# Another order for the last stage of the first pass, with six of eight next-norm tiles turned by DMA, filler products in the head, and the first weights loaded in two halves

## Time and profile before

| | us |
|---|---|
| three timed runs | 1172.57, 1175.30, 1181.07 (median 1175.3) |
| the profiled execution | 1170.05 |
| its span, slowest core (core 2) | 1168.3 |
| spans of the eight cores | 1163.5 to 1168.3 |
| granted TensorE clock, mean of each core | 0.996 to 0.998 |

### The profile page before, as it was taken

The page is one execution under the profiler, slowest core; times in us unless marked ns, Lnnn a source line. Parts: engine busy times, 40 slices in busy tenths (PEclk is TensorE's granted clock), DMA queues, the critical chain, the costliest instruction groups (busy, mean ns, idle before and its releaser), DMA issues.

```text
span 1168.3 us, 18289 instructions; the slowest of 8 cores (1163.5 to 1168.3 us)
## 1 busy us (share of the span) xinstructions
PE 1124.1 (96%) x6425; PEld 574.5 (49%) x6520; DVE 609.8 (52%) x668; ACT 384.7 (33%) x649; POOL 341.8 (29%) x451
## 2 busy tenths in 40 slices
PE   4999999999999999999899999999999999999996
PEld 2444454444444444443446666666644444444443
DVE  3267662123687776124615866322267888871247
ACT  3622221111354444014772223112133444430134
POOL 2411113222234434114832010222223333330144
PEclk9999999999999999999999999999999999999998
DMA  7983642544844333358699355244377343343443
GB/s 185 183 158 72 111 71 46 80 83 78 145 93 72 73 73 72 62 92 192 196 195 233 63 116 90 37 73 73 72 127 127 73 73 73 73 90 64 79 102 129
DMA packets 58585, 119.77 MB, mean 103 GB/s; under 512 B 33264, under 2 KB 34032, under 8 KB 55936
## 3 DMA queue, kind: packets, MB, share of 16 engines
q0 software_dynamic: 20112, 82.85, 40.9%
q1 hardware_dynamic: 38240, 35.58, 11.3%
q10 hardware_dynamic: 144, 0.17, 0.1%
HBM read 184.14 MB, written 9.95 MB: 166 GB/s over the span
## 4 chain that ended last, share of the span: by engine, by line
PE 88%; POOL 3%; issue 2%; DVE 2%; DMA 2%; ACT 1%; DVEq 0%; POOLq 0%; ACTq 0%; SPq 0%
PE pq L322 88%; POOL s_wd L335 2%; DMA s_ring<-wpk 1%; DVE s_wd L338 1%; ACT s_xnb L329 1%; POOL s_st_r L335 1%; POOL s_st_ss L335 1%; DMA s_h<-x 1%; ACT s_wd L329 0%; DVE s_h L338 0%; PE pq L326 0%; POOL s_R L335 0%; DVE s_xnb L510 0%; DVE s_xnb L338 0%; DVE s_xn L335 0%
## 5 line engine op out<-in xcount | busy, mean ns | idle before, releaser
L322 PE MATMUL pq<-s_xn,s_ring 128*128 128x512 bf16 (+3 forms) x3693 | 658.1, 334 | 4.2 <-DVE s_wd L338 0.8
L322 PEld LDWEIGHTS pq<-s_xn,s_ring 128*128 128x128 bf16 x3744 | 335.6, 98 | 313.2 <-issue 2.0
L338 DVE SCALAR_TENSOR_TENSOR s_wd<-pq,s_cst,s_wd 128x1023 f32<-128x1023 f32 (+1 forms) x176 | 225.2, 1282 | 63.1 <-ACT s_carry_f L332 53.8
L335 POOL TENSOR_TENSOR s_R<-s_wd 128x1024 bf16<-128x1024 f32 (+3 forms) x84 | 146.3, 1742 | 357.9 <-DVE s_wd L338 166.6
L322 PE MATMUL pq<-s_ring,s_R 128*128 128x512 bf16 x936 | 206.9, 379 | 2.7 <-DVE s_wd L338 1.4
L338 DVE SCALAR_TENSOR_TENSOR s_wd<-s_wd,pq 128x512 f32<-128x512 f32 (+4 forms) x98 | 66.7, 681 | 193.2 <-PE pq L322 170.4
L329 ACT ACTIVATE s_wd<-pq 128x512 f32<-128x512 f32 (+4 forms) x138 | 78.4, 568 | 240.1 <-PE pq L322 238.7
L329 ACT ACTIVATE s_wd<-pq,s_cst 128x1024 f32<-128x1024 f32 x88 | 98.1, 1114 | 165.5 <-PE pq L322 165.5
L322 PEld LDWEIGHTS pq<-s_ring,s_R 128*128 128x128 bf16 x960 | 93.2, 98 | 112.5 <-issue 1.8
L322 PE MATMUL pq<-s_R,s_ring 128*128 128x347 bf16 (+3 forms) x875 | 125.1, 292 | 0.3
L322 PE MATMUL pq<-s_ring,s_xn 128*128 128x512 bf16 (+1 forms) x514 | 119.6, 383 | 5.3 <-DMA s_ring<-wpk 3.3
(11 more groups left out here) (81 smaller groups left out, 483.6 us busy)
## 6 DMA issues: line engine op xcount, KB each, us to landing
s_ring<-wpk POOLq DMA_DIRECT2D x110, 512.0 KB, 8.9
s_ring<-wpk POOLq DMA_DIRECT2D x20, 1024.0 KB, 10.0
s_h<-x SPq DMA_DIRECT2D x16, 512.0 KB, 16.1
y<-s_wd SPq DMA_DIRECT2D x15, 512.0 KB, 2.7
s_R<-x SPq DMA_DIRECT2D x8, 512.0 KB, 9.2
s_ring<-wpk POOLq DMA_DIRECT2D x4, 768.0 KB, 7.2
s_gbc<-g_v SPq DMA_DIRECT2D x2, 512.0 KB, 15.0
s_gbc<-g_ffn SPq DMA_DIRECT2D x2, 512.0 KB, 6.3
```

The lines of the kernel that those rows point to most:

```text
L322: P.op("pe", lambda e: e.matmul(out, lhsT=lhsT, rhs=rhs, start=start, stop=stop), reads=reads, writes=writes, signal=signal)
L335: P.op(eng, lambda e: e.tensor_tensor(out=out, in0=in0, in1=in1, op=op), reads=reads, writes=writes)
L338: P.op("dve", lambda e: e.scalar_tensor_tensor(out=out, in0=in0, scalar=scalar, in1=in1, op0=op0, op1=op1), reads=reads, writes=writes)
```

## The change

It does four things. First, item 0 is loaded by two DMAs, one for each half of its landing area (four of the eight channel blocks each); the first half has a name of its own (`v0a`), products of item 0 wait for both, and tiles 2 and 3 are loaded when the first half has landed, the others each behind the tile two before. Second, 18 and 28 products of 128x128 with no use are put behind the transposes of tiles 0 and 1. Third, `WsT` and `Ds` are made on Pool instead of VectorE. Fourth, the last stage: `g_mix` is loaded into `gbc` ahead of the x tiles; next-norm tiles 0 to 5 are scaled with the gain on VectorE and transposed by DMA, tiles 6 and 7 scaled on VectorE and transposed on TensorE behind the stage; the pair of a y square comes behind the next tile's addition on Pool; the second pass's first slab may be loaded one tile earlier; and the order behind the stage is new. The pair's place also changes in the second pass, where the same function is used.

```diff
@@ Ring._try_load
-                P.dma("pool", (lambda e: e.dma_start(out=land, in_=wsrc)), f"wr{s}", writes=res)
+                if i == 0:
+
+                    for q, wr in ((0, ["v0a"]), (1, res)):
+                        P.dma("pool", (lambda e, q=q: e.dma_start(out=land[:, q * 2048:(q + 1) * 2048], in_=wsrc[:, q * 2048:(q + 1) * 2048])),
+                              "wv0a" if q == 0 else f"wr{s}", writes=wr)
+                else:
+                    P.dma("pool", (lambda e: e.dma_start(out=land, in_=wsrc)), f"wr{s}", writes=res)
...
-                self.item_slot[i] = (dst, res)
+                self.item_slot[i] = (dst, res + ["v0a"] if i == 0 else res)
@@ loads of h in the head
-        v0r = R.item_slot[0][1]
-        for t, after in ((2, [("h", 0)]), (3, v0r), (4, [("h", 1)] + v0r), (5, [("h", 2)]), (6, [("h", 3)]), (7, [("h", 4)])):
+        for t, after in ((2, ["v0a"]), (3, [("h", 1), "v0a"]), (4, [("h", 2)]), (5, [("h", 3)]), (6, [("h", 4)]), (7, [("h", 5)])):
@@ setup_spatial
-            TTT("dve", WsT[:], ws[:, 0:1024].rearrange("p (j t) -> p j t", j=8), bc_mid(tr[:, 0:128], 8), ALU.mult, [wsr, trr], ["WsT"])
+            TTT("pool", WsT[:], ws[:, 0:1024].rearrange("p (j t) -> p j t", j=8), bc_mid(tr[:, 0:128], 8), ALU.mult, [wsr, trr], ["WsT"])
...
-                P.op("dve", lambda e, j=j: e.tensor_scalar_mul(out=Ds[:, j, :], in0=idf[0:16, 0:16], scalar1=w00[0:16, j:j + 1]),
+                P.op("pool", lambda e, j=j: e.tensor_scalar_mul(out=Ds[:, j, :], in0=idf[0:16, 0:16], scalar1=w00[0:16, j:j + 1]),
@@ TileNorm: the pair leaves sq and becomes rstd; Pipe.push and the head call both
+            def rstd(self):
                 rstd_col(self.si, self.rows, 1 if self.gi else 0)
@@ the head
+        def warm(n):
+            pw, pwr = psR.at(5)
+            for q in range(n):
+                MM(pw[:, 0:128], ones[:], idb[:], True, True, ["ones", "idb"], pwr, q == n - 1)
+
         heads[0].tp()
+        warm(18)
         heads[1].tp()
+        warm(28)
         heads[2].scale()
@@ ahead of the last stage
             if pss == 0:
+                load_gain(g_mix)
                 for t in range(8):
                     load_xst(t)
@@ the last stage: y_sq without its pair, y_rstd has it
+            def y_rstd(rec):
+                rstd_col(rec[3], 128, 1)
...
+            def A_sq(t):
+                nxt.append(TileNorm(xst[t], ("xst", t), 128, t * 128, t, 0, dma=t < 6))
+                nxt[t].sq()
+                nxt[t].rstd()
...
-                if plus:
-                    normed.append(y_sq(plus.pop()))
+                prev = plus.pop() if plus else None
+                if prev:
+                    normed.append(y_sq(prev))
                 STT(tg[:, 0:D], tg[:, 0:D], 1.0, pE, ALU.add, ALU.mult, [tgr] + pEr, [tgr])
                 TTT("dve" if samp and t >= 4 else "pool", tg[:, 0:D], tg[:, 0:D], h[:, t, :], ALU.add, [tgr, ("h", t)], [tgr])
                 plus.append((t, tg, tgr))
+                if prev:
+                    y_rstd(normed[-1])
                 while len(normed) > (0 if samp and t >= 5 else 1):
                     y_out(normed.pop(0))
-                if pss == 0 and t == 2:
+                if pss == 0 and t == 1:
                     R.limit = len(ITEMS) + 2
                     R.prefetch()
                 if pss == 0 and t > 0:
-                    A_push(1, t - 1)
-                    if len(pipeA.q) > 2:
-                        pipeA.pop_tp(psR.at(7) if t < 5 else None)
+                    A_sq(t - 1)
+                if pss == 0 and t > 1:
+                    nxt[t - 2].scale()
...
             if pss == 0:
-                A_push(1, 7)
-                normed.append(y_sq(plus.pop()))
+                A_sq(7)
+                last = y_sq(plus.pop())
                 B_mm(1, 0, 8)
-                pipeA.scale()
+                nxt[6].scale()
+                y_rstd(last)
                 B_mm(1, 0, 0)
+                nxt[6].tp()
+                nxt[7].scale()
+                y_out(normed.pop(0))
                 for t in range(1, 8):
-                    if pipeA.q and t in (1, 2, 4):
-                        pipeA.pop_tp()
-                    if normed:
-                        y_out(normed.pop(0))
                     B_mm(1, 0, t)
+                    if t == 1:
+                        nxt[7].tp()
+                        y_out(last)
                     if t == 4:
                         R.limit = NIT
                         R.prefetch()
```

More of the change, by code:

```diff
@@ L215, in build_program @@
     cst_d = din("cst", [128, NCST]); tri_d = din("tri", [128, 128])
-    g_v = din("g_v", [D]); g_ffn = din("g_ffn", [D]); g_ple = din("g_ple", [D]); g_final = din("g_final", [D])
+    g_mix = din("g_mix", [D]); g_v = din("g_v", [D]); g_ffn = din("g_ffn", [D]); g_ple = din("g_ple", [D]); g_final = din("g_final", [D])
     wpk_d = din("wpk", [NWPK])
@@ L530, in push @@
                 tn.sq()
+                tn.rstd()
                 self.scale()
@@ L573, in sample_norm @@
             return finish
[L576 to L582, removed]
         vit = {}
@@ L619, in build_program @@
             heads[t].sq()
+            heads[t].rstd()
             if t == 5:
@@ L967, in y_sq @@
                 si = sumsq(tg[:, 0:D], [tgr], jk[:, :], jkr, 128)
-                rstd_col(si, 128, 1)
                 return (t, tg, tgr, si)
+            def y_rstd(rec):
+                rstd_col(rec[3], 128, 1)
             def y_out(rec):
@@ L1023, in build_program @@
             normed = []
+            nxt = []
+            def A_sq(t):
+                nxt.append(TileNorm(xst[t], ("xst", t), 128, t * 128, t, 0, dma=t < 6))
+                nxt[t].sq()
+                nxt[t].rstd()
             for t in range(8):
@@ L1141, in make_in_maps @@
     shared = {
-        "g_v": f(g_v[0]), "g_ffn": f(g_ffn[0]), "g_ple": f(g_ple[0]), "g_final": f(g_final), "cst": f(cst), "tri": np.triu(np.ones((128, 128), dtype=np.float32)),
+        "g_mix": f(g_mix[0]), "g_v": f(g_v[0]), "g_ffn": f(g_ffn[0]), "g_ple": f(g_ple[0]), "g_final": f(g_final), "cst": f(cst), "tri": np.triu(np.ones((128, 128), dtype=np.float32)),
         "wpk": wpk, "w_spatial": f(np.asarray(w_spatial[0]).transpose(2, 0, 1).reshape(128, 1024)), "b_spatial": f(b_spatial[0]),
```

## The result

The changed kernel takes 1194.8 us (median of five runs, 1192.8 to 1200.3), the kernel before 1175.3 beside it: a ratio of 1.0139, 95% interval [1.0103, 1.0175], so 16.3 us slower [12.1, 20.6]. The forecast was 1183 in a range that ended at 1191: the direction was right, the size half.

What follows compares the result with a forecast made beforehand. In the last stage, VectorE and Pool excluding each other were to bound the pace at 5.9 us a tile against TensorE's 4.3. Head -2.6 and stage +10.8 gave +8.2: 1178.2 profiled, 1183 on the timed scale, range 1167 to 1191.

Steps and rivals of the forecast that it cites:

- The sum: Whole kernel: head -2.6 and first pass's last stage +10.8 make +8.2 us on the profile.
- Head: Start of the kernel: second slab's products start at 36.5 instead of 39.05, -2.6 us (ends 0 and -3.7).
- the same 10.7: Head: second weight slab, issued at 25.8, takes 10.7 us as before and lands at 36.5.
- Moves at nothing: WsT work on Pool, earlier second-pass slab, the pair's new place in the second pass, SP order: all costed at 0.
- Step 1: Start of the first pass's last stage: the gain ahead of the x tiles delays them by 1.8 us.
- Step 2: First pass's last stage: VectorE scaling and Pool addition exclude each other, 5.9 us a tile; last gating +6.7.
- Rival 2: Last stage: TensorE's pace, but tile 3's square waits for tile 0's transpose, landing at 570; 1174 us, chance 0.10.
- the short turn: Last stage: scaling and addition run side by side, VectorE's turn is 3.8 us, TensorE sets the pace at 4.3.
- Step 3: End of the first pass's last stage: half ends at 605.1 against 596.4, +8.7, before the restart's +2.1.
- The restart: End of the stage: TensorE's transposes and first set run slower after some 9 us idle, +2.1 us.
- Rival 3: Last stage: TensorE's pace, but tile 5's transpose still queued when the next slab starts; 1181 to 1190, chance 0.05.

Runs made afterwards that it cites:

- after: The changed kernel with all parts of the change, against the kernel before: 1194.8 us, ratio 1.0139.
- the head alone: Kernel before with only halved first weights, new order of h loads, filler products, WsT and Ds on Pool: ratio 1.0011, 1.3 us slower than before.
- The pair back: Changed kernel with the y statistics pair ahead of Pool's addition again in the second pass: ratio 1.0117, 13.7 us slower than before.
- the gain behind two x tiles: Changed kernel with the pair ahead of the addition again in the second pass, gain loaded behind the first two x tiles: ratio 1.0112 against before.
- the scaling on ScalarE: Changed kernel with the six next-norm scalings on ScalarE, without the gain g_mix: ratio 1.0125, 14.6 us slower than before.
- with the fillers: Changed kernel, second-pass pair ahead of the addition again, 128 filler products ahead of tile 6's transposes: ratio 1.0107, 12.5 us slower than before.
- the additions on VectorE: Changed kernel, second-pass pair moved back, squares' unused outputs in PSUM, last stage's additions of h on VectorE: ratio 1.0162, 19.0 us slower than before.

## Why the prediction was wrong

The sum had +8.2 on the profile; the undisturbed cores show +17.3. Step by step:

- **Head, -2.6: -0.4 in after, +0.5 alone, neither to be told from nothing.** The step that failed is that the slab "lands after the same 10.7". In after tile 5 lands at 23.3 and the slab is issued at 25.6 (means of eight cores), both as forecast; but it takes 11.0 us and lands at 36.6, where before one issued at 26.5 took 10.0 and landed at 36.5. In the head alone not even the tiles came earlier (tile 5 at 24.1). And the forecast read one core for all: 39.05 is the second slab's start on core 2, while on cores 1, 3, 4 and 6 it started before 37 already, without a wait for the slab. Counting no gain for the fillers was right.
- **Moves at nothing: wrong by 4.0, the largest miss.** "Only a pair of small Pool instructions changes place, and TensorE sets that stage." The pair was also what kept Pool's addition behind VectorE's sample product; without it TensorE waits 1.58 and 0.65 to 0.80 us there, and on four of the six cores 16 products run at the lower clock for a while. I had the rule for the first pass's stage and did not apply it to the other stage that the same function writes. The pair back shows it.
- **Step 1, +1.8 at the start: 3.8.** The gain and the x tiles come in 3.8 us later, not 1.8. With the gain behind two x tiles the first lands as in before, so it is the gain, at nearly twice the price of its bytes.
- **Step 2, the turn of 5.9: right in kind, 5.62 in size.** An instruction starts up to 0.1 us before the one ahead of it ends, which the sum of durations leaves out. Five turns give 28.1, not 29.5; a wait for tile 0's transpose adds 2.3. So the last gating is 30.6 behind the third (30.4 with the pair back): the forecast's 29.5 is near it by luck, as two errors cancel.
- **Rival 2 was no rival but a second bound.** I gave it a chance only with the short turn. By the forecast's own figures it acts with the long one too: the landing was put at 570, and tile 3's square stands behind the fifth gating, at 554.1 + 2 x 5.9 = 565.9. It landed at 571.5 on core 0, and the square was due at 566.2. Take away the exclusion alone and it gives everything back (the scaling on ScalarE); take away the wait alone and 2.3 us come back; both, 6.9 at the last gating.
- **Step 3, the end: +4.1 forecast behind the last gating, +4.3 measured** (551.5 less 547.2 from it to the second mark). Tile 6's transposes start 8.35 behind that gating, where the forecast has 8.5. The restart is 1.1 by the fillers where I had 2.1, and the products behind it take longer than I added up (from tile 6's transposes to ScalarE's first tile of the other half 15.76 us with the fillers, 14.84 by the sum): two errors that cancel here too.
- **Rival 3** did not act in after, but not for the reason given. An empty queue is not what decides: with the additions on VectorE tiles 3's and 4's transposes took 3.1 and 3.0 on core 0, so the queue was as empty, and tile 5's took 21.0, since the slab was issued ahead of it. There the rival cost 10.3 us between the last gating and the second mark (562.1 against 551.8), near the 11 that it was given.

So of the 9.1 us that were missing, 4.0 are the pair, 2.2 the head, 2.0 the gain, and 0.9 the rest of the stage. The mechanism that the forecast staked most on, the turn of VectorE and Pool, is there; its price and the places where else the two meet were wrong.

## What to carry to other kernels

An exclusion between two engines has to be looked for wherever the two meet, and a small instruction between two big ones can be what decides who goes first: before moving it, list what becomes ready in its place. A rival that names another wait is not excluded because the forecast's own bound seems longer; work out by how much it is hidden, and expect it when the bound is taken away. And a kernel that keeps a small transfer clear of large ones only by being slow will show it when it gets faster.

## What the runs showed of the hardware

- A VectorE scaling of 128x1024 from one tensor, 0.75 us alone, takes 2.83 beside Pool's addition, as one with two SBUF sources does (3.37). A product of 128x128 takes 2.37 instead of 0.29.
- A DMA transpose of one tile takes 3.1 us when a 1 MB weight slab is issued 1.4 us behind it on another queue and four more of 0.5 MB come after its landing. It takes 19 to 24 when that slab is issued ahead of it and the four ahead or within 3 us behind. With all five issued 0.3 to 3 us behind it, it took 3.1 to 6.8 on four cores and 21 to 28 on four.
- A gain broadcast over the partitions, 0.5 MB as written, put the next tile back by 3.3 us (third gating at 247.3 against 244.0), where its share of the queue's bytes would have been 1.8.
